# Norm sums and outputs handed over per 128 channels, semaphores cleared in two parts, and first loads reordered over two queues

## The reference, cut to what matters

```python
def rms_norm(x, g):
    xf = x.astype(jnp.float32)
    y = xf * lax.rsqrt(jnp.mean(xf * xf, axis=-1, keepdims=True) + NORM_EPS)
    return (y * g.astype(jnp.float32)).astype(x.dtype)

def hybrid_layer(x, st, pos0, P, l):
    xn = rms_norm(x, P['ln1_g'][l])
    proj = (xn @ P['w_in'][l]).astype(jnp.float32)
    ...                                  # four mixers, gates, merged by channel
    x = x + merged @ P['w_out'][l]
    x = x + peer_ffn(rms_norm(x, P['ln2_g'][l]), P['peer_w_q'][l], P['peer_keys'][l],
                     P['peer_u'][l], P['peer_v'][l])

def run_trunk(x, states, pos0, P):
    for l in range(DEPTH):               # DEPTH = 2
        x, st_new = hybrid_layer(x, st, pos0, P, l)
    return rms_norm(x, P['lnf_g']), ...
```

## Time and profile before

| | us |
|---|---|
| median of 3 runs (2459.05 to 2464.91) | 2464.0 |
| the profiled execution, its own time | 2461.85 |
| its span, first to last instruction | 2460.0 |
| PE matmul busy | 2041.2 |
| DVE busy | 1444.3 |
| POOL busy | 648.2 |
| ACT busy | 586.9 |

### The profile page before, as it was taken

One profiled execution on the slowest core, in us unless ns is written; L12 is line 12 of the kernel. 1 busy time (PEld: TensorE's weight loads), 2 busy tenths in 40 slices (PEclk: granted clock), 3 DMA queues, 4 the chain that ended last, 5 costly groups with the idle time before them and its releaser, 6 DMA issues.

```text
span 2460.0 us, 23902 instructions
## 1 busy us (share of the span) xinstructions
PE 2041.2 (83%) x7108; PEld 1238.0 (50%) x7108; DVE 1444.3 (59%) x3574; ACT 586.9 (24%) x1572; POOL 648.2 (26%) x677
## 2 busy tenths in 40 slices
PE   5999989987787887878789898898977778777876
PEld 4778778763333333323368787786633333333323
DVE  1336355438878777785423354643588786777754
ACT  0221132022222222222222202220333223222221
POOL 0400000014444444434112000000244454444440
PEclk9999999999889888989989999999988989988898
DMA  5320123349999999999653201334499999999994
GB/s 231 120 104 1 73 91 124 131 170 396 397 421 416 407 421 421 409 421 407 283 191 121 70 1 73 114 128 163 182 420 396 420 416 415 421 415 408 412 422 196
DMA packets 101903, 665.99 MB, mean 271 GB/s; under 512 B 20224, under 2 KB 21792, under 8 KB 21792
## 3 DMA queue, kind: packets, MB, share of 16 engines
q0 software_dynamic: 76032, 553.68, 54.7%
q1 hardware_dynamic: 24352, 110.38, 12.3%
q10 hardware_dynamic: 1408, 0.66, 0.1%
HBM read 657.97 MB, written 6.71 MB: 270 GB/s over the span
## 4 chain that ended last, share of the span: by engine, by line
PE 50%; DMA 25%; DVE 14%; issue 6%; ACT 3%; POOL 1%; another core or an unknown queue 1%; SPq 0%; DVEq 0%; POOLq 0%; ACTq 0%
DMA arena<-in_uv,arena 24%; PE ps L871 17%; PE ps L499 9%; PE ps L558 6%; PE ps L837 3%; PE ps L821 2%; PE ps L807 2%; DVE ring L1717 1%; PE ps L481 1%; PE ps L639 1%; PE ps L642 1%; ACT arena L1154 1%; DVE arena L1430 1%; PE ps L633 1%
## 5 line engine op out<-in xcount | busy, mean ns | idle before, releaser
L871 PE MATMUL ps<-ring,arena 128*128 128x512 f32 x1056 | 565.7, 690 | 223.3 <-ACT arena L1154 223.2
L871 PE MATMUL ps<-arena 128*128 128x512 f32 x1056 | 487.6, 602 | 47.6 <-ACT arena L1154 47.5
L871 PEld LDWEIGHTS ps<-ring,arena 128*128 128x128 f32 x1056 | 226.1, 222 | 560.5 <-ACT arena L1154 322.9
L1717 DVE SCALAR_TENSOR_TENSOR arena<-arena 128x1024 f32<-128x1024 f32 x264 | 323.5, 1225 | 226.4 <-DMA arena<-in_uv,arena 226.3
L1247 POOL DMA_INDIRECT ring<-in_uv,arena x264 | 291.7, 1105 | 479.1 <-PE ps L871 441.4
L1717 DVE SCALAR_TENSOR_TENSOR ring<-ring,arena 128x1024 f32<-128x1024 f32 x264 | 322.6, 1222 | 123.6 <-DMA ring<-in_uv,arena 90.7
L871 PEld LDWEIGHTS ps<-arena 128*128 128x128 f32 x1056 | 192.0, 189 | 335.9 <-issue 194.6
L1247 POOL DMA_INDIRECT arena<-in_uv,arena x264 | 271.8, 1030 | 250.9 <-PE ps L871 199.3
L1152 ACT ACTIVATE arena<-arena 128x1 f32<-128x1 f32 x528 | 107.1, 203 | 912.6 <-DVE ring L1717 486.1
L558 PE MATMUL ps<-xn,ring 128*128 128x264 f32 x1024 | 246.4, 400 | 15.1 <-ACTq L1103 9.3
L499 PE MATMUL ps<-xn,ring 128*128 128x264 f32 x1024 | 237.8, 393 | 13.7 <-remote 13.7
(11 more groups left out here) (396 smaller groups left out, 1979.4 us busy)
## 6 DMA issues: line engine op xcount, KB each, us to landing
ring<-in_w SPq DMA_DIRECT2D x88, 1024.0 KB, 4.8
ring<-in_uv,arena POOLq DMA_INDIRECT x264, 10.5
arena<-in_uv,arena POOLq DMA_INDIRECT x264, 13.8
st<-in_st SPq DMA_DIRECT2D x2, 2048.0 KB
out_st<-st SPq DMA_DIRECT2D x2, 2048.0 KB
const<-in_const SPq DMA_DIRECT2D x1, 3181.0 KB, 12.0
arena<-in_keys SPq DMA_DIRECT2D x2, 1024.0 KB, 10.6
x<-in_x SPq DMA_DIRECT2D x1, 1056.0 KB, 5.0
```

Of the source, the lines that this page charges most:

```text
L871: m = mm(bank(2 * tt + half, 512), dg[:, k, :], row(k)[:, D + 512 * half:D + 512 * half + 512], start=False, stop=False, skip_group_check= ...
L1717: stt(u, u, 1.0, xtok[:, tt, :], ALU.mult, ALU.mult, accum_out=hid[:, k:k + 1]).then_inc(S("dve_hid"), 1)
```

## The change

Seven edits, all in the order and the hand-over of work. No arithmetic of the result changes.

1. DVE squares each 128 channels in an instruction of its own, with an increment of `dve_sq` each, and PE's sums wait for each of them.
2. In the second norm of a layer this happens inside the output projection: DVE squares a tile right behind its addition to `x`, and PE puts the sum of tile o - 2 behind the projection's tile o. The sums go to bank 2, the squares to `fg8`.
3. Each product of a norm increments `dve_xn`, and the first tile of PE's next stage waits for each of them.
4. SP clears 70 of now 89 per-layer semaphores after the last wait of its layer's transfers and the first `pe_acc`, before it waits for `arrive`; the other 19 (`LATE`) after it.
5. The first 260 of 6362 columns of `const` (`ident`, `ones`, `eps`) are loaded with `x` on SP's queue, `glob` and the other columns on ACT's queue; those other columns have a semaphore of their own, `act_const`, for which PE waits ahead of its column tiles.
6. `par` has a semaphore of its own, `sp_ln`, for which DVE waits ahead of the first norm's products.
7. The first four blocks of weights are issued right behind `par`, ahead of the eight other tensors.

```diff
@@ constants @@
+FIRST = CONST_AT["eps"][0] + 4
+LATE = ("dve_hid act_dg pe_acc pe_xa act_acc act_top dve_top dve_route sp_sw sp_sr act_ps pe_ps pe_wq act_step pe_step "
+        "sp_out sp_rw sp_hfin sp_dfin").split()
@@ sync @@
             e.dma_start(x[:, :, :], A["x"]).then_inc(S("sp_once"), 16)
-            e.dma_start(const[:, :], A["const"]).then_inc(S("sp_once"), 16)
-            e.dma_start(glob[:, :], A["glob"]).then_inc(S("sp_once"), 16)
+            e.dma_start(const[:, 0:FIRST], A["const"][:, 0:FIRST]).then_inc(S("sp_once"), 16)
...
+                e.dma_start(par[:, :], lay("par").rearrange("a p c -> p (a c)")).then_inc(S("sp_ln"), 16)
...
+                for n in range(4):
+                    block_of(n % 4, l * N_BLOCKS + n)
...
-                for n in range(20):
+                for n in range(4, 20):
                     block_of(n % 4, l * N_BLOCKS + n)
...
                 e.wait_ge(S("sp_dfin"), 48)
+                e.wait_ge(S("pe_acc"), 1)
+                for name in sems:
+                    if name not in LATE:
+                        e.sem_clear(sems[name])
                 e.wait_ge(arrive, 4)
                 e.sem_clear(arrive)
-                for s in sems.values():
-                    e.sem_clear(s)
+                for name in LATE:
+                    e.sem_clear(sems[name])
@@ tensor @@
-            def sum_squares(sq_, k):
-
-                e.wait_ge(S("dve_sq"), k)
-                for kt in range(KT):
-                    i = mm(bank(0), C("ones"), sq_[:, kt, :], start=kt == 0, stop=kt == KT - 1)
-                i.then_inc(S("pe_ss"), 1)
+            def sum_square(k, kt):
+
+                e.wait_ge(S("dve_sq"), KT * (k - 1) + kt + 1)
+                i = mm(bank(2), C("ones"), (sqs if k == 1 else sqs2)[:, kt, :], start=kt == 0, stop=kt == KT - 1)
+                if kt == KT - 1:
+                    i.then_inc(S("pe_ss"), 1)
...
                     for kt in range(KT):
+                        if t == 0:
+                            e.wait_ge(S("dve_xn"), kt + 1)
                         at = b * D + kt * P
...
                         m.then_inc(S(tag), 1)
+                        if o >= 2:
+                            sum_square(2, o - 2)
+                    for kt in range(KT - 2, KT):
+                        sum_square(2, kt)
 
                 project(merged, "pe_wo", "dve_x")
-                sum_squares(sqs, 2)
-                e.wait_ge(S("dve_xn"), 2)
 
                 e.wait_ge(S("sp_keys"), 16)
@@ scalar @@
+            e.dma_start(glob[:, :], A["glob"]).then_inc(S("sp_once"), 16)
+            e.dma_start(const[:, FIRST:NCONST], A["const"][:, FIRST:NCONST]).then_inc(S("act_const"), 16)
             e.wait_ge(S("sp_once"), 48)
@@ vector @@
-            def squares(sq_):
-                tt_(sq_[:, :, :], x[:, :, :], x[:, :, :], ALU.mult).then_inc(S("dve_sq"), 1)
+            def square(kt, to):
+                tt_(to[:, kt, :], x[:, kt, :], x[:, kt, :], ALU.mult).then_inc(S("dve_sq"), 1)
...
                 for kt in range(KT):
-                    i = stt(xn[:, kt, :], x[:, kt, :], gain(kt), rstd, ALU.mult, ALU.mult)
-                i.then_inc(S("dve_xn"), 1)
+                    stt(xn[:, kt, :], x[:, kt, :], gain(kt), rstd, ALU.mult, ALU.mult).then_inc(S("dve_xn"), 1)
...
-                e.wait_ge(S("sp_par"), 16 * 9)
+                e.wait_ge(S("sp_ln"), 16)
                 norm(1, lambda kt: V("ln1", kt))
...
                     if o % 2:
                         e.sem_inc(w_free[o // 2], 1)
-
-                e.wait_ge(S("dve_x"), KT)
-                squares(sqs)
+                    e.wait_ge(S("dve_x"), o + 1)
+                    square(o, sqs2)
+
                 norm(2, lambda kt: V("ln2", kt))
```

More of the change, by code:

```diff
@@ L86, in constants @@
     t["ones"] = np.ones((P, P))
+    t["eps"] = np.tile([NORM_EPS, RWKV_EPS, HEAD_EPS, 1.0], (P, 1))
     t["headsum"] = (head[:, None] == head[None]).astype(np.float64)
@@ L136, in constants @@
     t["zero"] = np.zeros((P, SEQ))
-    t["eps"] = np.tile([NORM_EPS, RWKV_EPS, HEAD_EPS, 1.0], (P, 1))
     at, n = {}, 0
@@ L281, in build @@
         merged = carve(8, N, at=mix)
+        sqs2 = fg8
         side = ring[:, 4, 0:7 * N].rearrange("p (a b) -> p a b", b=N)
@@ L336, in build @@
                 "pool_hg pool_hy pool_kz "
-                "sp_dfin sp_hfin sp_keys sp_out sp_par sp_rw sp_sr sp_svr sp_svw sp_sw ").split():
+                "sp_dfin sp_hfin sp_keys sp_ln sp_out sp_par sp_rw sp_sr sp_svr sp_svw sp_sw ").split():
             sem(name)
-        once = {name: sem(name, False) for name in ("sp_once", "pool_zero", "dve_lb", "act_lb")}
+        once = {name: sem(name, False) for name in ("sp_once", "act_const", "pool_zero", "dve_lb", "act_lb")}
         def S(name):
@@ L398, in lay, with block_of @@
                     return A[name][bass.ds(l, 1)]
[L400 to L403, removed]
+                e.dma_start(par[:, :], lay("par").rearrange("a p c -> p (a c)")).then_inc(S("sp_ln"), 16)
+                def block_of(j, n):
+                    take(e, w_free[j], 1)
+                    e.dma_start(ring[:, j, :], A["w"][bass.ds(n, 1)].rearrange("a p c -> p (a c)")).then_inc(w_full[j], 16)
+                for n in range(4):
+                    block_of(n % 4, l * N_BLOCKS + n)
+                for dst, name in ((wa_up[:, :], "wa_up"), (g_up[:, :], "g_up"), (w_if[:, :, :].rearrange("p a b -> p (a b)"), "w_if"),
+                                  (st[:, :, :, :].rearrange("p a b c -> p (a b c)"), "st"), (st_n[:, :], "st_n"),
                                   (st_shift[:, :, :].rearrange("p a b -> p (a b)"), "st_shift"),
@@ L406, in _ @@
                     e.dma_start(dst, lay(name).rearrange("a p c -> p (a c)")).then_inc(S("sp_par"), 16)
-                def block_of(j, n):
-                    take(e, w_free[j], 1)
-                    e.dma_start(ring[:, j, :], A["w"][bass.ds(n, 1)].rearrange("a p c -> p (a c)")).then_inc(w_full[j], 16)
-                for n in range(20):
+                for n in range(4, 20):
                     block_of(n % 4, l * N_BLOCKS + n)
@@ L487, in _ @@
             with e.Fori(0, L) as l:
-                sum_squares(sqs, 1)
-                e.wait_ge(S("dve_xn"), 1)
+                for kt in range(KT):
+                    sum_square(1, kt)
                 def column_tile(t):
@@ L502, in _ @@
                 nothing = C("zero", P)
+                e.wait_ge(S("act_const"), 16)
                 def head_sum(j):
@@ L544, in _ @@
                         mm(bank(6, 512), nothing, const[:, 0:512], start=False, stop=True, skip_group_check=True).then_inc(S("pe_step"), 1)
-                e.wait_ge(S("sp_par"), 16 * 9)
+                e.wait_ge(S("sp_ln"), 16)
+                e.wait_ge(S("sp_par"), 16 * 8)
                 products = iter([(g, kt) for g in range(32) for kt in range(KT)])
@@ L835, in _ @@
                         for kt in range(KT):
+                            if o == 0:
+                                e.wait_ge(S("dve_xn"), KT + kt + 1)
                             at = (o % 2) * D + kt * P
@@ L924, in root @@
                 e.wait_ge(S("pe_ss"), k)
-                act(to, bank(0), ACT.Sqrt, bias=eps(0), scale=1.0 / D).then_inc(S("act_rt"), 1)
+                act(to, bank(2), ACT.Sqrt, bias=eps(0), scale=1.0 / D).then_inc(S("act_rt"), 1)
+            e.dma_start(glob[:, :], A["glob"]).then_inc(S("sp_once"), 16)
+            e.dma_start(const[:, FIRST:NCONST], A["const"][:, FIRST:NCONST]).then_inc(S("act_const"), 16)
             e.wait_ge(S("sp_once"), 48)
@@ L1299, in _ @@
                 own.clear()
-                squares(sqs)
-                e.wait_ge(S("sp_par"), 16 * 9)
+                for kt in range(KT):
+                    square(kt, sqs)
+                e.wait_ge(S("sp_ln"), 16)
                 norm(1, lambda kt: V("ln1", kt))
+                e.wait_ge(S("act_const"), 16)
                 own(ts(lb[:, 0, :], lb_all[:, bass.ds(l * PR, PR)], 1e-30, None, ALU.max))
@@ L1624, in _ @@
                         e.sem_inc(w_free[o // 2], 1)
-                e.wait_ge(S("dve_x"), KT)
-                squares(sqs)
+                    e.wait_ge(S("dve_x"), o + 1)
+                    square(o, sqs2)
                 norm(2, lambda kt: V("ln2", kt))
-                e.wait_ge(S("dve_xn"), 2)
+                e.wait_ge(S("dve_xn"), 2 * KT)
                 own(e.memset(qz, 0.0))
```

2 lines of the change are left out of this document (1 added, 1 removed).

## The result

The changed kernel takes 2442.6 us (median of 4 runs, 2438.68 to 2446.06) against 2464.45 before (4 runs, 2459.05 to 2466.01): a ratio of 0.9915, 95% interval 0.9893 to 0.9936. The forecast was 2444.5, with 2436 to 2451 as its range. The profiled execution took 2446.06 us with a span of 2444.2; against that of before it is 15.8 us shorter, where the sum said 18.3.

The account below looks back on a forecast made before the run. The serial chain, chiefly experts and tiles, bounds the kernel, with norms and layer turn as seams. Start -5.8, turn and layer 2's first norm -10.2, last norm -5.7, second norms +3.4: -18.3 us; forecast 2444.5, range 2436 to 2451.

Parts of the forecast that it names:

- Clears: Between the layers and after layer 2: 69 fewer semaphore clears behind the wait for `arrive`, 3.8 us gained twice.
- Squares in eight: First norm of each layer and last norm: PE starts its sums earlier, 1.9 us gained in each of three.
- Products one by one: First norm of both layers: PE starts after the first product, 2.8 us gained; nothing in the last norm.
- `sp_ln`: First norm of layer 2: `par` no longer waits for the last of nine loads, 1.7 us gained; none in layer 1.
- Four blocks ahead: Weight blocks issued before eight tensors delay those by some 10 us, but they are needed much later: cost nothing.
- The start over two queues: Kernel start: `x` and first columns on one queue, the rest on another, taking turns by rows: 1.1 us gained.
- The rival by bytes: Kernel start: queues share by bytes, so the start gains 3.5 us more, 2441 us; chance 0.13.
- The packet rule: Kernel start: an engine drains 9 to 17 descriptors from one ring before turning; estimated gain 0.5 instead of 1.1 us.
- The second norms: Sums inside the projection delay its end and the landing of `keys`: losses of 1.9 us and 1.5 us (layer 2).
- The clock: PE's clock after idle gaps at the norms: no change taken, 1.5 us either way for each in the range.
- the last norm: End of the kernel: 3.8 us from clears and 1.9 from squares, 5.7 us gained together.

Follow-up runs that it names:

- e5: Kernel before, with only the early clears added (69 of 88 semaphores cleared during the experts): 2456.16 us, ratio 0.9969.
- e7: Changed kernel with ACT's two transfers swapped, the large part of `const` first and `glob` behind it: 2445.39 us, ratio 0.9919.
- e3: Changed kernel with the large part of `const` on SP's queue behind `x` and the first columns: 2436.86 us, ratio 0.9894.
- e1: Changed kernel with the load of `keys` moved ahead of the four `w_q` blocks on SP's queue: 2426.98 us, ratio 0.9842.
- e6: Kernel before, with `keys` loaded ahead of the `w_q` blocks: 2463.67 us, ratio 0.9994.
- e2: Changed kernel with all eight sums of the second norm behind the projection again: 2440.48 us, ratio 0.9903.
- e8: Changed kernel plus early `keys`, large `const` part on SP's queue, and five extra matmuls behind the sums of each layer's two norms: 2415.69 us.
- e10: The kernel of e8 run once more: 2410.13 us, ratio 0.9781.

## Why the prediction was right, step by step

*Clears*: 3.8 us twice were counted; 4.15 and 3.86 came, and 3.9 twice in e5. *Squares in eight*: 1.9, measured 1.94, 1.93 and 1.94. *Products one by one*: 2.8, measured 3.05 and 3.04, from reciprocal to tile. *`sp_ln`*: 1.7, measured 1.63. *Four blocks ahead*: nothing, and no wait on weights or on the eight tensors appears.

*The start over two queues*: 1.1 us were counted, 1.94 came. The price was off, and for a reason that the working missed: it let the long rows meet `x`, but `glob` goes first on ACT's queue and shields it. In e7 the long rows do meet `x`, as the working had it, and DVE starts at 13.81, no earlier than the 13.64 of before: so that 1.1 came near to what was measured is luck. That rows take turns was right (e3, e7), though the row it was read from was thin: of the four kinds of 4 KB transfer in the experts of the kernel before one landed in 1.5 us and three in 5.3 to 6.5. The rival by bytes is out. The packet rule that the prediction cited from the Trainium skill, "DMA: Bandwidth & Descriptors", "Queues, rings and completion order", does not agree with these runs if a packet is the eight of 128 rows that each of the 16 engines of the profile gets of such a transfer: in the changed kernel the first columns would then land behind the whole rest, but they land 1.9 us ahead of it (11.6 against 13.5), and in e7 `x` and the rest end within 0.3 us of each other.

*The second norms*: +1.9 and +1.5 were counted, +2.17 and +1.71 measured, with PE's wait ended by the landing of `keys` at 499.2. e1 shows that `keys` were the cause, e6 that this wait was hidden before, e2 that the sums' length passes straight into it.

*The clock* was put at no change. It moved single terms: the last norm gained 5.0 instead of 5.7 since its sums took 6.25 us instead of 5.5, and the column tiles took 28.80 in both layers instead of 30.18 and 30.85. The first two `w_q` tiles took 9.80 and 10.05 instead of 8.99 and 10.43. The seams' measured terms add up to -7.4 - 10.8 - 5.0 + 3.9 = -19.3, where -18.3 was forecast. The spans differ by 15.8 because the stretches outside the seams gave 3.5 back: 2.2 us in the first layer from the start of the column tiles to the projection, 0.9 in its experts, 0.3 in layer 2. The 2.2 is the clock again. The column tiles gained 1.4, but the stretch behind them lost 3.3: in the changed kernel the granted clock is 0.50 from about 136 to 142 us, while PE is busy all the time, and 96 column matmuls took 23.06 us instead of 21.36. In layer 1 of the kernel before it stays at 1.00 there; its layer 2 has the same loss (23.13 us). The chain before, layer 1:

```profile
146.40 21.36 PE ps L499 x96
```

None of the edits touches these stretches, so I take them as the spread between executions; what makes the clock fall in one of them and not in the other is open. The medians moved by 21.9, so single profiles and medians bracket the sum. That the median came within 2 us of the forecast is partly luck: runs of the changed kernel alone spread over 7 us. What the profiles confirm is the terms.

## What to carry to other kernels

When a hand-over gets shorter, look for the wait that ends next, and count its landing from what releases it. Here it ended 0.5 us ahead of the old one, and moving one load was worth nothing before the change and 16 us after it. Short transfers that many engines wait for belong at the head of one queue; beside long rows on a second queue each of their rows waited for a long one here. A gap of 3 us on TensorE can cost as much again in clock behind it, and profiles of one execution then differ by more than the edit under test.

## What the runs showed of the hardware

- Two hardware queues alternate row by row, here with rows of 48 bytes, 1, 8 and 24 KB. 130 KB landed 10.4 us after issue beside 24 KB rows on the other queue, 5.1 where both were in one queue (e3); 1056 KB in 12.3 us beside long rows, 4.9 beside rows of 48 bytes.
- After 3.0 us of idleness the same program finds TensorE's clock at either level: 28.8 or 31.8 us for 128 matmuls of 128x264, once 30.3, in fourteen layers. It was the upper level where the 16 sums just ahead had taken at most 6.16 us, and the lower where they had taken 6.19 or more. After 0.8 to 0.9 us it was at the upper level in all eight gaps of e8 and e10. It also fell with PE busy throughout, for 6 us from 136 us on in the changed kernel's first layer.
- A semaphore cleared by SP costs 0.056 us (88 in 4.9 us; 69 fewer gave 3.9 in e5). The restart of DVE's loop behind `go` shows as 3.78 us in the chain of before and 3.50 in that of the changed kernel, so it did not grow when four 1 MB loads were issued in the middle of it.
